# The same work in another order on VectorE: low weights, conv taps, drained halves and copies in the attention stage, and two sums of the front, of a transformer layer

## The reference

```python
h = rms_norm(x, g_pre_mix)
hc, bg, cg, q, k, v = split(h @ w_in, 6)                  # 512 columns each
u = cg * hc                                               # short causal conv of 3 taps
y_conv = bg * (u[-2] * w0 + u[-1] * w1 + u * w2)          # shifts along the rows
scores = (q / 8) @ k.T + rel_bias                         # 8 heads of 64, chunks of 64 rows,
o = softmax(scores) @ v                                   # each sees itself and 8 chunks before
y = concat(group_rms_norm(y_conv), group_rms_norm(o)) @ w_out
x = x + rms_norm(y)
f = (silu(rms_norm(x) @ w_gate) * (rms_norm(x) @ w_up)) @ w_ffn_out
out = x + rms_norm(f)
```

## Time and profile before

| | us |
|---|---|
| median of 3 runs | 1124.7 (1124.58 to 1124.71) |
| profiled execution, its own time | 1124.3 |
| its span | 1122.5 |
| mean granted clock of TensorE | 0.994 |
| busy: DVE, ACT, POOL | 783.2, 475.3, 152.7 |

### The profile page before, as it was taken

One profiled execution on the slowest core, in us unless ns is written; L12 is line 12 of the kernel. 1 busy time (PEld: TensorE's weight loads), 2 busy tenths in 40 slices (PEclk: granted clock), 3 DMA queues, 4 the chain that ended last, 5 costly groups with the idle time before them and its releaser, 6 DMA issues.

```text
span 1122.5 us, 15903 instructions
## 1 busy us (share of the span) xinstructions
PE 1095.6 (98%) x5581; PEld 907.2 (81%) x5581; DVE 783.2 (70%) x1229; ACT 475.3 (42%) x827; POOL 152.7 (14%) x256
## 2 busy tenths in 40 slices
PE   9999999999988999999999999999999999999997
PEld 7888877787766788888888888888888888888886
DVE  6878887455646557786878787777778777555584
ACT  6532253466643655663332322222323257444441
POOL 3300000001101112210122112211211120000031
PEclk9999999999989999999999999999999999999999
DMA  7332213700020155342564446445634699777632
GB/s 277 104 125 59 75 57 115 242 20 20 20 75 1 56 208 188 131 132 81 173 215 157 131 142 215 139 119 172 195 122 143 214 309 377 242 228 227 217 116 84
DMA packets 116758, 166.20 MB, mean 148 GB/s; under 512 B 7816, under 2 KB 73368, under 8 KB 116704
## 3 DMA queue, kind: packets, MB, share of 16 engines
q1 hardware_dynamic: 99072, 105.40, 29.3%
q0 software_dynamic: 16464, 55.89, 14.5%
q10 hardware_dynamic: 1168, 4.20, 1.0%
HBM read 120.60 MB, written 47.99 MB: 150 GB/s over the span
## 4 chain that ended last, share of the span: by engine, by line
PE 73%; DVE 1%; ACT 1%; issue 1%; DVEq 0%; POOL 0%; POOLq 0%; ACTq 0%
PE psum L1344 34%; PE psum L1371 18%; PE psum L1228 8%; PE psum L935 7%; PE psum L978 2%; PE psum L949 1%; PE psum L959 1%; PE psum L924 1%; ACT arena L1616 0%; PE psum L1065 0%; PE psum L986 0%; PE psum L968 0%; DVE arena L2292 0%; PE psum L1072 0%; ACT arena L1625 0%
## 5 line engine op out<-in xcount | busy, mean ns | idle before, releaser
L1344 PE MATMUL psum<-arena_r,ws 128*128 128x512 f32 x960 | 224.1, 389 | 0.0
L1344 PEld LDWEIGHTS psum<-arena_r,ws 128*128 128x128 f32 x960 | 180.2, 188 | 37.4
L1344 PE MATMUL psum<-hT,ws 128*128 128x512 f32 x720 | 169.9, 389 | 0.0
L1344 PEld LDWEIGHTS psum<-hT,ws 128*128 128x128 f32 x720 | 135.1, 188 | 28.0
L1371 PE MATMUL psum<-hT 128*128 128x512 f32 (+1 forms) x600 | 135.2, 385 | 0.0
L1371 PEld LDWEIGHTS psum<-hT 128*128 128x128 f32 x600 | 111.3, 188 | 22.5
L935 PE MATMUL psum<-hT,ws 128*128 128x512 f32 (+1 forms) x528 | 122.4, 382 | 2.7 <-DVE arena L2292 1.9
L935 PEld LDWEIGHTS psum<-hT,ws 128*128 128x128 f32 x528 | 90.5, 190 | 23.8 <-issue 7.4
L2541 DVE TENSOR_TENSOR misc<-misc,psum 128x512 f32<-128x512 f32 x100 | 68.6, 686 | 47.2 <-PE psum L1344 44.9
L1836 ACT ACTIVATE ws<-o_raw 128x512 fp32r<-128x512 f32 x40 | 25.1, 628 | 138.0 <-DVE o_raw L2519 137.5
L1228 PE MATMUL psum<-ws,hT 128*128 128x512 f32 x348 | 81.7, 392 | 0.0
(11 more groups left out here) (275 smaller groups left out, 1567.6 us busy)
## 6 DMA issues: line engine op xcount, KB each, us to landing
raw<-in_w_ffn_in SPq DMA_DIRECT2D x44, 512.0 KB, 4.1
act_scratch<-arena POOLq DMA_DIRECT2D x77, 256.0 KB, 3.2
raw<-in_w_in SPq DMA_DIRECT2D x22, 512.0 KB, 3.8
arena<-in_w_ffn_out POOLq DMA_DIRECT2D x22, 512.0 KB, 5.6
arena<-act_scratch SPq DMA_DIRECT2D x38, 256.0 KB, 3.4
arena<-in_x SPq DMA_DIRECT2D x16, 512.0 KB, 6.5
raw<-in_w_out SPq DMA_DIRECT2D x16, 512.0 KB, 3.5
raw<-act_scratch SPq DMA_DIRECT2D x26, 256.0 KB, 3.3
```

Source lines behind the costliest of these rows:

```text
L1344: last = mm(blocks(bank), w[:, k * P:(k + 1) * P], b_operand(i, part, k), start=fresh_bank and k == 0 and w is hi and part == 0, stop=k == ...
```

## The change

Both kernels do the same arithmetic on the same tiles; the order of instructions within the queues of PE, ACT and DVE differs.

- *Front*: DVE's `bank_sum(5, 6)`, with its wait for `conv_stored[0]`, stands before `mix_row(2)` and two low parts instead of behind them; `stats(1)` stands behind product 1 of round 5 instead of product 0, and ACT's `front_copy_first(5)` ahead of `conv_roots(1)`.
- *Scores*: tiles 0 and 1 are scored together in step 0 in every pair (before: in pairs 1 and 2 only). In pair 0 they stand ahead of that step's piece.
- *Pieces*: pairs take 10, 10, 12 and 12 instead of 11, 11, 10 and 12. In step 3 the piece stands ahead of `output`. At the end of pair 3 one piece stands ahead of the last `transpose_p` and one behind (before: two behind).
- *DVE*: `drain` stands behind `copy_o`, and at a pair's end ahead of `low_k`. `low_in(g)` runs one step later than ACT's high part. The three taps run one in each of the steps after half 9, at the step's end.
- `turn_back` in step 1 stands ahead of the wait for the exps.

```diff
@@ -507,9 +507,9 @@
-            if s == 2 or s == 0 and 0 < t < LAST:
+            if s in (0, 2):
                 return (s, s + 1)
-            return () if s == 3 or s == 1 and 0 < t < LAST else (s,) if s < NT else ()
+            return () if s in (1, 3) else (s,) if s < NT else ()
@@ -521,7 +521,7 @@
-        FILLS = [[1, 1, 1, 1, 2, 1, 1, 1, 2], [1, 1, 1, 1, 1, 1, 1, 2, 2], [1, 1, 1, 1, 2, 1, 1, 1, 1], [1, 1, 2, 1, 1, 2, 1, 1, 2]]
+        FILLS = [[1, 1, 1, 1, 1, 1, 1, 1, 2], [1, 1, 1, 1, 1, 1, 1, 1, 2], [1, 1, 1, 1, 2, 1, 1, 2, 2], [1, 1, 2, 1, 1, 1, 1, 2, 1, 1]]
@@ -531,11 +531,16 @@
-                         if pieces_ahead(t, s) <= q < pieces_ahead(t, s) + FILLS[t][s]), -1)
+                         if pieces_ahead(t, s) <= q < pieces_ahead(t, s) + FILLS[t][s]),
+                        -1 if q < AHEAD else STEPS * PAIRS - 1)
...
+        def taps_done(t, s):
+            return [n for n in range(TAPS) if step_of(8 * CG + 7) + n + 1 == STEPS * t + s]
@@ -1014,16 +1019,23 @@
             def step(t, s):
+                if s == 0 and t > 0:
+                    fill(t, s)
                 if s == 0:
-                    fill(t, s)
                     pe.wait_ge(qk_ready, t * 2 + 2)
...
                         scores(t, i)
+                if s == 0 and t == 0:
+                    fill(t, s)
                 if s == 0 and t > 0:
                     output(t - 1, NT - 2)
+                if s == 0:
+                    return
+                if s == 3:
+                    fill(t, s)
                 if s == 3 and t == 0:
                     pe.wait_ge(v_back, 64)
                 if s in (3, 5, 7):
@@ -1031,10 +1043,10 @@
-                if s == 0:
-                    return
-                if s < NT or t < LAST:
+                if s != 3:
                     fill(t, s)
+                if s == 1 and t > 0:
+                    turn_back(t - 1, NT - 2)
                 pe.wait_ge(exp_done, unit(t, 2 * s))
@@ -1042,14 +1054,12 @@
-                if s == 1 and t > 0:
-                    turn_back(t - 1, NT - 2)
                 transpose_p(t, s - 1)
...
                 if s == NT and t == LAST:
-                    fill(t, s)
+                    fill(t, NT + 1)
                     output(t, NT - 2)
@@ -1197,7 +1207,7 @@
-            behind = {(4, 2): 0, (5, 0): 1, (5, 5): 2}
+            behind = {(4, 2): 0, (5, 1): 1, (5, 5): 2}
@@ -1583,7 +1593,7 @@
-            conv_roots(1, PP[2]), front_copy_first(5), square_y(2)
+            front_copy_first(5), conv_roots(1, PP[2]), square_y(2)
@@ -2214,11 +2224,11 @@
                 if n == 5:
+                    dve.wait_ge(conv_stored[0], 16)
+                bank_sum(n, 6, tiles_of(q_row, 1), blocks(u2), blocks(BANK[3]), c12_made)
+                if n == 5:
                     mix_row(2)
                 front_low(n + 1, 4), front_low(n + 1, 5)
-                if n == 5:
-                    dve.wait_ge(conv_stored[0], 16)
-                bank_sum(n, 6, tiles_of(q_row, 1), blocks(u2), blocks(BANK[3]), c12_made)
                 front_low(n + 1, 6)
@@ -2308,8 +2318,6 @@
                         read_half(h // 2, h % 2)
-                        if h == 2 * CG + 1:
-                            tap(LAST, 0), tap(LAST, 1), tap(LAST, 2)
@@ -2318,19 +2326,19 @@
+                if s == 0 or s == NT and more:
+                    drain(t, s)
                 if s == NT and more:
                     low_k(t)
-                if s == 0:
-                    drain(t, s)
                 if s < NT:
                     add_bias(t, 2 * s)
                     add_bias(t, 2 * s + 1)
-                if 0 < s < NT:
-                    drain(t, s)
...
                 if s in (3, 5, 7):
                     copy_o(t, s - 3)
+                if 0 < s < NT:
+                    drain(t, s)
@@ -2348,21 +2356,20 @@
                     read_o(t, s - 3)
+                for n in taps_done(t, s):
+                    tap(LAST, n)
...
-                for g in chunks_next(t, s):
+                for g in chunks_next(t, s - 1):
                     low_in(g)
```

More of the change, by code:

```diff
@@ L2362, in step @@
                     copy_o(t, NT - 2)
-                else:
-                    drain(t, s)
-                if not more:
                     drain(t, s)
```

## The result

The changed kernel took **1106.0 us** (median of 4 runs, 1105.86 to 1106.28) against 1124.65 (1124.58 to 1124.71, 4 runs): a ratio of 0.9835, 95% interval 0.9818 to 0.9852, 18.6 us faster. The forecast was 1108.5 us in a range of 1104.5 to 1114.0. Of the rivals A came true, in the lower half of its own range. The profiled execution took 1106.1 us with a span of 1104.3, 18.2 less than before.

A forecast was written before the change was run, and what follows sets the result against it. TensorE, busy 1095.6 of 1122.5 us, bounds the kernel; waits in the attention stage are a matter of order. 1124.3 - 19.3 removed + 3.1 added = 1108.1, against the median 1108.5 us; range 1104.5 to 1114.

The forecast's parts named there:

- A: The forecast itself as a rival: 1105.5 to 1110.5 us, chance 0.52.
- Front sums: Before product 3 of round 6 and at `stats(1)`: DVE's sum moved ahead removes PE waits, 2.1 us together.
- Opening: Pair 0's start: scores 0 and 1 together ahead of the filler piece remove waits on ACT's copy and biases, 1.8 us.
- step 3: A piece ahead of P times V in step 3 removes waits for ACT's copy of the turned probabilities, 3.5 us.
- exps: PE's two waits on exps, in pair 2 and at the end of pair 3, covered by pieces: 0.7 us together.
- Copies ahead of drains and low parts: The three waits of `turn_back` for `copy_o`, longest in pair 3 behind the conv taps, all go: 3.2 us.
- Low weights later: Pair 2, step 6: DVE's low part one step later no longer delays the biases that scores 7 need, 2.1 us.
- Drain ahead of low_k: End of pair 2: drain ahead of `low_k`, both pieces of that half a step before, removes a wait of 1.9 us.
- The clock: Attention stage: three low-clock stretches beside PE waits of about 2 us go with the waits, 4.0 us of at most 4.5.
- The factor chain: Added: `copy_o` to `read_o`, 6.9 us against 5.7 of PE work, a wait of 1.25 in pairs 1 and 3, 2.5 us.
- Bank: Added: pair 3, step 3, the moved piece starts a half before DVE has drained the half before, 0.4 us.
- Rival B: The clock dips stay or move to the new waits: 1112.5 us, chance 0.15.

The follow-up runs named there:

- run 9: The changed kernel with the three edits of the front undone, the rest kept: 1108.66 us.
- run 11: The changed kernel with DVE's drain ahead of `copy_o` again, both behind the biases: 1106.04 us.
- run 10: The changed kernel with the three conv taps run at once behind the drain of their half, as before the change: 1108.34 us.
- run 4: The changed kernel with DVE's low parts back in the step of ACT's high parts: 1115.56 us.
- run 3: The changed kernel with two pieces in step 4 of pairs 1 and 3 and low parts one step later: 1106.65 us.
- run 8: The changed kernel with two pieces in step 4 of pairs 1 and 3, low parts a step later, last copies of P moved ahead: 1102.44 us.
- run 2: The changed kernel with each low part and conv tap one step later, away from POOL's power: 1105.45 us.
- run 12: Run 8 with pair 3's opening low part one step further and the first tap just ahead of `o_scale` in step 4: 1101.51 us.

## Why the prediction was right, step by step

The direction and the mechanism held: PE's waits in the attention stage were a matter of DVE's and ACT's order, and all that was won there came through, as nothing behind the stage changed. By the steps of the sum:

- **Front sums** (2.1): PE's filler started 2.21 earlier, and undoing it costs 2.3 to 2.6 (run 9). Right.
- **Opening, step 3, exps** (1.8, 3.5, 0.7): all those waits are gone, and the end of pair 3 kept 1.02, where some 0.9 was forecast. Before, step 3 of pair 0 looked like this on PE's timeline:

```profile
214.69 0.60 PE L959 MATMUL psum<-ident,arena 128*128 128x128 f32 x4
216.02 0.44 PE L978 MATMUL psum<-misc,arena 128*64 128x128 f32 x4 [0.73 <-issue]
```

The four transposes ahead of P times V gave some 0.7 us more than the waits behind them: before, 1.33 us went by from their start to P times V's, 0.60 of it busy and 0.73 waiting, and now the piece starts 0.35 after them (246.87, 247.22). A busy time whose end is modelled hides a quarter of a us (0.60 less 0.35), in pairs 0, 1 and 2; in pair 3 the new wait on the bank takes it. I had counted only the waits.
- **Copies ahead of drains and low parts** (3.2): the sum is right, its ground in part wrong. The new place of the drain behind `copy_o` is worth nothing (run 11), since no half that DVE drains ends in steps 3, 5 or 7 of the new FILLS. The pair 3 wait went with the taps (run 10: 2.05 back), though in the changed kernel 1.58 us of waiting stand at that pair's `read_o` in its place; the others went with the low parts (run 4) and, I take it without an own run, with the half that FILLS moved by a step.
- **Low weights later** (2.1): undersized as an edit. In the new order they cost 9.5 if left where they were, 4.7 of it waiting and the rest the clock. The sum was not touched by that, as it counted only what the old order lost.
- **Drain ahead of low_k** (1.9): the wait of 1.9 is gone. Not tried alone.
- **The clock** (4.0): **the mis-sized term**. With at most 4.5 I had left out two stretches, 320 to 325 and 355 to 360 us, whose granted clocks were 0.89 and 0.98; with them the lost clock is 5.2 us (0.55 and 0.1 more than the 4.5). Each of the three dips then lost 1.7 (1.2 + 0.55, 1.7, 1.6 + 0.1). PE's busy time fell by 6.7: the 5.2, the transposes' 0.7, and 0.8 that I can't place. The two stretches, of the kernel before:

```profile
320.00:325.00 5.00, 5.00 (x49) 4.52 (x46) 0.86 (x3) 0.46 (x2) 0.00 (x0) 0.89 0.00 0
...
355.00:360.00 5.00, 4.96 (x54) 4.14 (x53) 3.35 (x8) 2.75 (x5) 0.13 (x1) 0.98 0.01 3
```

How many dips the kernel before has is partly chance: of its 21 executions beside the experiments 15 took 1122.5 to 1123.4 us, some 1.7 less than the four of the result, with a mean clock of 0.995 to 0.997. Against those 15 the change wins about 16.8 us and not 18.6. So one dip of the clock term, 1.7 us, was luck: it depends on which executions of the kernel before are compared.

- **The factor chain** (2.5 added): 1.75 and 1.58, and 0.27 on the biases ahead of the first, 3.6. The path was forecast at 6.9 and is 6.8 and 6.8 without POOL's delays of 0.94 and 0.38; the work beside it was right too. What I missed is that low part 3 and tap 0, put "where DVE waits for POOL anyway", slow POOL itself, as they start just ahead of the power.
- **Bank** (0.4) and **low part 2** (0.15): 0.44, and nothing seen.

So the net of 16.2 became 18.2: 1.2 from the clock, 0.7 from the transposes, 1.1 the other way for the chain's excess, 0.8 in busy time that I can't place, and the rest, 0.4, in small waits (part 3 of the sum had let 0.4 on L1625 in step 7 stand, and that is gone too). The recorded chances add up to 1.01 (0.96, 0.02 and 0.03), a slip that changes nothing here. Rival B was weighed by the right question with the wrong premise. The dips did follow the waits (none in the profiled run once waits were under 1.8), but a wait is a chance of a dip, not a cause that always works, which is also why the kernel before scatters over 2 us and the changed one over 0.4 in most of its runs.

## What to carry to other kernels

When a piece of cover is moved ahead of a wait, price the wait that it leaves behind in the same sum: here 3.5 us won and about 3 lost. A second piece alone did not make it pay (run 3); it did together with the other moves of run 8. Before an order is tuned further, look for the one instruction that waits at the head of an in-order queue for another engine (the low part, 4.53 us idle with biases and copies behind it): its place was worth more than any other single edit that was undone, 9.5 us with the clock in it. Sum lost clock over every stretch whose granted clock is under 1, not only over those that catch the eye, and treat waits of 1.7 us and more as carrying a chance of 1.7 us on top, what each dip lost here. When an edit brings a wait back, compare PE's idle time as well as the total: in runs 4 and 10 half of the loss and more was the clock. And keep a long DVE instruction from starting just ahead of a POOL instruction that DVE will wait for; here one that started 1.5 us into it did no harm.

## What the runs showed of the hardware

- **The granted clock** fell behind PE waits of 1.74, 1.92, 2.05, 2.14, 3.04 and 3.26 us, and stayed at 1.00 behind others of 1.72, 1.75, 1.88, 1.92 (run 4, 323.39) and 2.84, one of them the same wait of the same instruction in another execution. The Trainium skill, "TensorE: Matmul & The Clock Gate" (Part 1: the HAM clock gate), says that the monitor's window runs freely, whatever the kernel does; that agrees with the chance seen here. The table of the two states in the same part ties the low level to TensorE being idle before; here the length of the idling alone did not decide, since 2.84 left the clock high and 1.74 did not. The section "A second HAM failure mode" of that page of the Trainium skill has frequent short idling between groups of matmuls move the clock between its levels, and that agrees.
- **POOL is held up by a DVE instruction that is already running.** A power of 16 columns took 2.90 to 2.92 us all four times in the kernel before and twice in the changed one. There it took 3.84 where a DVE subtraction of 1.22 us with two SBUF inputs had started 0.17 before it, and 3.28 where a tap of 0.74 with one had started 0.22 before it: 0.94 and 0.38 more, with 1.05 and 0.52 us left of the DVE instruction. With both moved away (run 2) the powers take 2.92 and 2.90. Where the DVE instruction starts later, the power keeps its 2.90: in run 12 the tap starts 1.59 into it, and in the changed kernel a subtraction of 1.23 (370.86) starts 1.51 into pair 3's last power (369.35), and neither DVE instruction is longer for it. The Trainium skill, "GPSIMD Engine Reference" (its table of the engine, the row on SBUF interfaces), says that the two engines share these, with contention where DVE has two SBUF inputs or runs in a 2-port mode. The runs agree for the subtraction and give it a price; whether the tap ran in such a mode no run here shows, and the row does not say which instruction has to start first.
- **A short matmul group's busy time is not its distance.** Four transposes show 0.60 busy, and the next group can start 0.35 after theirs.
